# Input projection of a hybrid decoder step: one sweep over w_in for the u columns and the first token tile, with the bias products behind it

## The reference

```
h = rmsnorm(x);  [q | k | v | u] = h @ w_in          # 1024 x 2048
A: 8 heads x 64, dilated window attention (128,1), (512,4), (2048,16),
   T5 relative bias (32 buckets), branches merged by their denominators
B: u in 4 channel groups, trailing mean over 2/4/8/16 positions minus the token,
   then a 128 x 128 map per group and a scale per channel
x += [A | B] @ w_out
x += cross attention (4 heads x 256) into 256 memory tokens
x += top-4-of-32 mixture of experts (clamped SwiGLU)
y = rmsnorm(x)
```

## Time and profile before

| what | us |
|---|---|
| median of 3 runs | 1463.88 |
| lowest, highest | 1461.9, 1466.05 |
| profiled execution, its own time | 1460.94 |
| span in its profile | 1459.1 |
| TensorE busy | 1277.7 (88%) |
| VectorE busy | 479.7 (33%) |
| ScalarE busy | 238.5 (16%) |
| GpSimd busy | 65.2 (4%) |
| bytes moved by DMA | 562.83 MB, mean 386 GB/s |

### The profile page before, as it was taken

One profiled execution on the slowest core, in us unless ns is written; L12 is line 12 of the kernel. 1 busy time (PEld: TensorE's weight loads), 2 busy tenths in 40 slices (PEclk: granted clock), 3 DMA queues, 4 the chain that ended last, 5 costly groups with the idle time before them and its releaser, 6 DMA issues.

```text
span 1459.1 us, 16484 instructions
## 1 busy us (share of the span) xinstructions
PE 1277.7 (88%) x6397; PEld 532.2 (36%) x6397; DVE 479.7 (33%) x1025; ACT 238.5 (16%) x467; POOL 65.2 (4%) x64
## 2 busy tenths in 40 slices
PE   7985978899779499998999899988999999989986
PEld 4352333347554433333333233333333333333332
DVE  2038999531512621321321222212212232123124
ACT  2135343220321200110111010010010001001102
POOL 1010000002202400000000000000000000000000
PEclk9985988899989699999999999999999999999999
DMA  9988698799979979999999999999999999999993
GB/s 350 344 277 355 270 364 345 299 357 371 338 289 394 336 304 430 426 428 427 427 429 428 429 429 427 429 429 428 429 428 429 429 428 429 429 428 429 428 429 158
DMA packets 51212, 562.83 MB, mean 386 GB/s; under 512 B 6501, under 2 KB 8645, under 8 KB 20349
## 3 DMA queue, kind: packets, MB, share of 16 engines
q1 hardware_dynamic: 49589, 557.16, 93.6%
q0 software_dynamic: 1584, 5.13, 0.9%
HBM read 556.15 MB, written 73.28 MB: 431 GB/s over the span
## 4 chain that ended last, share of the span: by engine, by line
DMA 48%; PE 39%; DVE 10%; ACT 1%; issue 1%; SPq 0%; DVEq 0%; ACTq 0%
DMA wide<-in_w_gate_up 47%; PE bank L1777 12%; PE bank L1491 4%; PE bank L1384 3%; PE bank L1512 3%; PE bank L1801 2%; PE bank L1598 2%; PE bank L1534 2%; DVE small L1113 2%; DVE wide L1110 1%; PE bank L1400 1%; PE bank L1478 1%; PE bank L1586 1%; PE bank L1649 1%; DVE wide L1111 1%
## 5 line engine op out<-in xcount | busy, mean ns | idle before, releaser
L1777 PE MATMUL bank<-wide,att 128*64 128x512 f32 x2048 | 463.2, 596 | 59.2 <-DMA wide<-in_w_gate_up 59.2
L1777 PEld LDWEIGHTS bank<-wide,att 128*64 128x64 f32 x2048 | 139.8, 136 | 363.4 <-issue 228.5
L1801 PE MATMUL bank<-slim,att 128*64 128x512 f32 x1024 | 226.8, 595 | 0.0
L1306 DVE TENSOR_SCALAR att<-bank 128x512 f32<-128x512 f32 x32 | 22.1, 692 | 470.1 <-PE bank L1777 470.1
L1801 PEld LDWEIGHTS bank<-slim,att 128*64 128x64 f32 x1024 | 70.6, 137 | 152.2 <-issue 149.2
L1285 DVE TENSOR_TENSOR x<-x,bank 128x512 f32<-128x512 f32 x68 | 46.6, 686 | 236.6 <-PE bank L1759 226.4
L913 ACT ACTIVATE att<-att 128x512 f32<-128x512 f32 x32 | 20.2, 630 | 529.5 <-DVE att L1306 529.5
L1759 PE MATMUL bank<-tb,att 128*128 128x512 f32 (+1 forms) x192 | 84.7, 611 | 1.8 <-ACT tb L922 1.3
L922 ACT ACTIVATE tb<-bank 64x512 f32<-64x512 f32 x64 | 37.8, 591 | 234.1 <-PE bank L1801 233.7
L1512 PE MATMUL bank<-slim,ta 128*128 128x512 f32 x128 | 58.2, 608 | 0.0
L1113 DVE TENSOR_REDUCE small<-wide 128x24 f32<-128x1536 f32 x32 | 56.1, 1753 | 1.1
(11 more groups left out here) (269 smaller groups left out, 1132.6 us busy)
## 6 DMA issues: line engine op xcount, KB each, us to landing
wide<-in_w_gate_up SPq DMA_DIRECT2D x128, 2048.0 KB, 25.5
slim<-in_w_down SPq DMA_DIRECT2D x64, 2048.0 KB, 22.0
out_k_win_sample<-in_cache_k_win SPq DMA_DIRECT2D x16, 2044.0 KB, 23.7
out_v_win_sample<-in_cache_v_win SPq DMA_DIRECT2D x16, 2044.0 KB, 29.0
wide<-in_cache_k_win SPq DMA_DIRECT2D x16, 1024.0 KB, 9.1
wide<-in_cache_v_win SPq DMA_DIRECT2D x16, 1024.0 KB, 6.8
wide<-in_w_in SPq DMA_DIRECT2D x8, 1024.0 KB, 14.9
wide<-in_cache_mem_k SPq DMA_DIRECT2D x8, 1024.0 KB, 19.9
```

Source lines behind the costliest of these rows:

```text
L1777: ins = M(bk[half[h], :], rows[:, k, :], wide[:, k, c:c + 512], start=False, stop=k == KC - 1)
L1801: ins = M(bank_y[half[h], :], aT[:, f % 4, f // 4, :], slim[:, f, 512 * h:512 * h + 512], start=f == 0, stop=f == KC - 1)
```

## The change

- **Order of PE.** The transposes come first. Then one sweep over k makes the four `u` groups and the three `qkv` products of tile 0 together. Behind it stand `bias_w`, `bias_f`, `state`, all eight `toep`, `qkv` of the samples, and last `qkv` of tile 1. `trq`, `trk`, `fresh`, `utp`, `uts` and `pool` follow as before, without `state` between them.
- **ACT** copies in the order of the jobs. It makes `qrows` when the last product of tile 1 is there (they lie on columns of `wide` that hold `w_in`), then copies tile 1 out.
- **DVE** normalises and scales before it spreads the bias table. The pooling sums stand before the split of `qrows`.
- **`rbrep`** lies in `att` in place of `scr`, which the pooling sums use.
- **SP** loads x first and `w_in` before the bias constants. The windows wait for `qkv` of tile 1 in place of `u` 3. `COPIES` begins with 5, 4 in place of 7, 2: two copies, not four, stand between the Toeplitz table and the windows, and four, not two, behind the windows.

```diff
-        rbrep = scr[0:33, 0:1024].rearrange("p (h n) -> p h n", n=P)
+        rbrep = att[0:33, 4608:5632].rearrange("p (h n) -> p h n", n=P)
...
-        add("bias_w"), add("bias_f")
         for t in range(3):
             for h in range(2):
                 add("tr1", t, h)
-        for t in range(2):
-            for c in range(3):
-                add("qkv", t, c)
-            for h in range(4):
-                add("toep", 4 * t + h)
-        add("qkv", 2)
         for c in range(4):
             add("u", c)
+        for c in range(3):
+            add("qkv", 0, c)
+        add("bias_w"), add("bias_f"), add("state")
+        for h in range(HEADS):
+            add("toep", h)
+        add("qkv", 2)
+        for c in range(3):
+            add("qkv", 1, c)
...
-        COPIES = [7, 2, 1, 1, 1, 1, 1, 1, 2, 5, 2, 2, 6]
+        COPIES = [5, 4, 1, 1, 1, 1, 1, 1, 2, 5, 2, 2, 6]
...
         def _(sp):
-            load(sp, "ident", ident[:, :], i["c_ident"])
             for t, (t0, n) in enumerate(TOK):
...
+            load(sp, "ident", ident[:, :], i["c_ident"])
+            load(sp, "gcol", gcol[:, :, :], i["g_all"])
             load(sp, "rel", rb[0:BUCKETS, :], i["rel_bias"])
+            for k in range(KC):
+                sp.dma_start(wide[:, k, :], w_in[k]).then_inc(wide_in[k], 16)
             load(sp, "cbias", cb[:, 0:TOEP + 6 * P + 4 * NS], i["c_bias"])
...
-            b, use = place(("u", 3))
+            b, use = place(("qkv", 1, 2))
             sp.wait_ge(bank_full[b], use + 1)
...
+            rows_out(0)
+            ps, s = product(act, "state")
...
+            for h in range(HEADS):
+                ps, s = product(act, "toep", h)
...
+            read_out(act, "qkv", 2)
+            b_, use = place(("qkv", 1, 2))
+            act.wait_ge(bank_full[b_], use + 1)
             for c in range(3):
                 ins = A(qrows[NS * c:NS * c + NS, :], qn[0:NS, 2, :], ACT.Copy)
             ins.then_inc(qrows_in, 1)
+            rows_out(1)
...
+            for k in range(KC):
+                pe.wait_ge(wide_in[k], 16)
+                for c in range(4):
+                    ins = M(tu[c][0][:, 0:T], wide[:, k, 1536 + P * c:1536 + P * c + P], ta[:, k, :], start=k == 0, stop=k == KC - 1)
...
+                for c in range(3):
+                    ins = M(tk[c][0][:, :], ta[:, k, 0:P], wide[:, k, 512 * c:512 * c + 512], start=k == 0, stop=k == KC - 1)
...
```

More of the change, by code:

```diff
@@ L261, in build @@
         add("fresh", 0), add("fresh", 1)
-        add("state"), add("utp"), add("uts")
+        add("utp"), add("uts")
         for g in range(4):
             add("pool", g)
-        COPIES = [7, 2, 1, 1, 1, 1, 1, 1, 2, 5, 2, 2, 6]
+        COPIES = [5, 4, 1, 1, 1, 1, 1, 1, 2, 5, 2, 2, 6]
         ROUND_AT = {3: 1, 7: 2}
@@ L724, in _, with rows_out @@
                 root(t, n, x[0:n, t, :], hn[0:n, t, :])
[L726 to L729, removed]
+            def rows_out(t):
                 for c in range(3):
@@ L732, in _ @@
                     A(qkvn[:, c, t, :], ps[:, :], ACT.Copy, scale=HD ** -0.5 if c == 0 else 1.0).then_inc(s, 1)
[L733 to L736, removed]
             for c in range(4):
@@ L998, in _ @@
             ins.then_inc(s, 1)
[L999 to L1016, removed]
             dve.wait_ge(loaded["cfirst"], 16)
@@ L1038, in _ @@
                 dve.sem_inc(pooled, 1)
+            dve.wait_ge(qrows_in, 1)
+            for c in range(3):
+                V.tensor_copy(rowsel[NS * c:NS * c + NS, :], ident[NS * c:NS * c + NS, NS * c:NS * c + NS])
+            link(V.tensor_copy(qparts, qrows))
+            for c in (1, 2):
+                r = slice(NS * c, NS * c + NS)
+                link(V.tensor_tensor(qrows[r, :], qrows[r, :], qparts[r, :], ALU.subtract))
+                link(V.tensor_copy(qparts[r, :], qrows[r, :]))
+            link(V.tensor_tensor(qrows[64:96, :], qrows[64:96, :], qparts[64:96, :], ALU.subtract))
+            V.tensor_copy(qparts[64:96, :], qrows[64:96, :]).then_inc(qparts_in, 1)
+            for h in range(2):
+                ps, s = product(dve, "fresh", h)
+                dst = bfr[:, :, :, :].rearrange("p b t (c h) -> p h c (b t)", h=2)[:, h]
+                V.tensor_tensor(dst, dst, ps[0:NS, 0:128].rearrange("p (c q) -> p c q", q=NS), ALU.add).then_inc(s, 1)
             dve.wait_ge(loaded["toep"], 16)
@@ L1363, in _ @@
             ins.then_inc(s, 1)
[L1364 to L1391, removed]
+            pe.wait_ge(loaded["state"], 16)
+            ps, s = take(pe, "state")
+            ns = DEC_B * STATE
+            for c in range(4):
+                ins = TR(ps[:, ns * c:ns * c + ns], state[:, P * c:P * c + P], ident[0:ns, 0:ns])
+            ins.then_inc(s, 1)
+            for h in range(HEADS):
+                ps, s = take(pe, "toep", h)
+                M(ps[:, 0:TOEP], rbrep[:, h, :], cb[:, 0:TOEP], start=True, stop=True).then_inc(s, 1)
             ps, s = take(pe, "qkv", 2)
@@ L1396, in _ @@
             ins.then_inc(s, 1)
[L1397 to L1401, removed]
+            tk = [take(pe, "qkv", 1, c) for c in range(3)]
+            for k in range(KC):
+                for c in range(3):
+                    ins = M(tk[c][0][:, :], ta[:, k, P:2 * P], wide[:, k, 512 * c:512 * c + 512], start=k == 0, stop=k == KC - 1)
+                    if k == KC - 1:
+                        ins.then_inc(tk[c][1], 1)
             for t, (t0, n) in enumerate(TOK):
@@ L1414, in _ @@
                 ins.then_inc(s, 1)
[L1415 to L1420, removed]
             for c in range(4):
```

38 lines of the change are left out of this document (30 added, 8 removed).

## The result

Against 1462.39 us before (median of 8 runs, 1458.06 to 1466.05), the changed kernel took **1469.92 us** (median of 8, 1466.0 to 1472.0): a ratio of 1.0045, 95% interval 1.0027 to 1.0063, 7.5 us slower by the medians.

The account below looks back on a forecast made before the run. The compute chain up to the second expert's weights was taken as the bound. Projection ending 1.4 us later but the loop starting 2.4 us earlier gave 1461.5 us against the 1463.88 median, range 1456.0 to 1467.0.

Parts of the forecast that it names:

- Start of the sweep: Projection on TensorE: would start at 17.0 us, not 19.7, as VectorE normalises before spreading the bias table: -2.7 us.
- Cold start: First part of the projection: TensorE would begin at 1.2 GHz after idling, costing 2.0 us (0 to 3.4).
- Bias products at full clock: Bias products moved into TensorE's stream would take 3.4 us, against 5.8 us at half clock before.
- No cost of alternating `u` and `qkv`: In the projection sweep, alternating these two products was taken to cost nothing (up to 3 us).
- Pooling hidden: Pooling sums on VectorE, about 10 us, would run beside the `qkv` products and end before 80 us, at no cost.
- E: End of the last projection product on TensorE: 93.1 us before, forecast at 94.5 (about 91 to 98).
- The key window as the new wait in front of the loop: Before the sample loop: window landing at 115.7 us would replace pooling as the wait; loop starts at 118.3, 2.4 earlier.
- Toeplitz in one piece, -1.0: On TensorE, the eight Toeplitz products without alternation would save 1.0 us (0 to 2) of 7.3.
- Copies ... I take 0: Two more copies behind the windows take some 12 us of DMA slack; loss for sequence 2's keys taken as 0.
- rival B: Copies delay sequence 2's keys and sequence 1's values, losing 2 to 4 us: 1463.5 to 1465 us; chance 0.15.
- the base: The kernel before's end of the last projection product, read as 93.1 us from one profile, from which shifts were counted.
- Rival C: Pooling stores land late behind copies in flight, moving SP's wait and the loop by 15 us: 1478.9 us; chance 0.13.

Follow-up runs that it names:

- copies_7_2: Changed kernel with COPIES back at 7, 2 (four copies ahead of the windows, two behind): 1461.8 us, ratio 1.000 against the kernel before.
- padded_7_2: Changed kernel with COPIES at 7, 2 and Toeplitz products on 128 rows, the added rows zero: 1455.36 us, ratio 0.9956.
- toep_128_rows: Changed kernel with Toeplitz products reading 128 rows of other operands, leaving out the Toeplitz bias: 1464.31 us in a single run.
- toep_alternate: Changed kernel with Toeplitz products alternating with the samples' rows and tile 1, not in one piece: 1473.4 us, ratio 1.0085.
- before_copies_5_4: Kernel before with only the table of copies changed to 5, 4: 1462.32 us, ratio 1.0004.
- wfc_5_4: Changed kernel, COPIES at 5, 4, with window requests and all four copies ahead of SP's wait for the pooling stores: 1458.49 us, ratio 0.9976.

## Why the prediction was wrong

**Right.** Start of the sweep (16.84 against 17.0). Cold start: the granted clock is 0.50 from 17 to 20 us, and the first eight `u` products took 3.85 us and not 1.94, that is 1.9 for a term of 2.0. (Its upper bound, half of 7 us, came from no row; copies_7_2 lost some 3.3, with 4.18 and 3.77 us for the first two groups.) Bias products at full clock (2.77 + 0.41 for 3.4). No cost of alternating `u` and `qkv` (1.94 + 2.58 us in each later step). Pooling hidden, over at 70. SP awake, at the load ahead of the first window request, 12.1 us behind E (11.7; the prediction took that load for the request itself). The key window as the new wait in front of the loop, also that it was hidden before.

**Wrong, step "Toeplitz in one piece, -1.0", and with it the samples' rows at an unchanged price.** The Toeplitz products took 3.8 us more and not 1.0 less: 10.54 in place of 6.7 in the chain (the 7.3 of the earlier trace rows are busy time, in which neighbours overlap). Reading a cost of alternating from that row was not the fault. At half clock 10.54 us are, as an estimate, 5.3 us of work at the full clock, so one piece does pack better. The fault was to take the full clock for given once PE was busy, for every product behind the start of the sweep. A piece of bias, state and 33-row Toeplitz products kept it at 0.50 for 17 us, also over the first of the samples' rows (9.62 in place of 7.00). Against the sum these two are 4.8 and 2.6 us too much, all other terms together 1.9 too little, and the 5.5 us between E = 94.5 and 100.0 remain. padded_7_2 gives them back. The Trainium skill, TensorE: Matmul & The Clock Gate, Part 1, says that "activity releases the throttle". If activity is read as the profile's busy time, this trace does not agree: PE was busy all the time and the clock stayed low, and the same products on 128 rows released it.

**Wrong, step "Copies ... I take 0".** It cost 8.1 us (6.6 by the ratios). What happened is rival B, to which I gave 2 to 4 us and a chance of 0.15. The step took mean DMA shares of 0.43 and 0.45 as room for two copies. It did not reckon the row of DMAs through: six window halves, four copies and the two halves of the keys of sequence 2 are 16.4 MB, and SP asks for them in one order. From the first window request to the landing of these keys it was 48.3 us in the change (112.5 to 160.8), 48.4 in toep_128_rows (106.6 to 154.9) and 47.3 in toep_alternate (114.9 to 162.2). The keys are used 31.5 us behind the start of the loop (120.68 and 152.14 in the earlier trace rows). So, where all these transfers follow each other without a pause, the keys are late if the loop starts less than 16.8 us behind the request. In the change it starts 10.2 behind it, in toep_128_rows 10.0, in toep_alternate 10.2, and the late keys wait 6.75, 6.95 and 5.67 us. In before_copies_5_4 it starts 17.1 behind, in wfc_5_4 20.5: no wait. The prediction had both numbers, a request at 106.2 and a loop at 118.3, only 12.1 apart: by the 48.3 us measured since, the four copies were 4.7 us too much even at my own E. That the new kernel makes the window the last wait is the same fact as that it has no room behind it; I forecast the one and did not draw the other.

**Wrong, the base.** I set E = 93.1 as the start of before. Two other profiles have 95.2 and 96.0, with a cold start of the projection. Against these copies_7_2 loses 3.7 to 4.5 us at E (99.7) and wins 4.5 between E and the loop (23.0 in place of 27.6), which is why it comes out at 1.000 while its loop starts 2.0 us behind that of the earlier trace rows. Its 1461.8 us stand next to the forecast of 1461.5, but by luck: E was 5 us later than in the sum, the window landed 7.9 us after SP woke and not 9.5, and the base was 2 to 3 us too early.

**Rival C** did not happen in the change: the store took 2.5 us, for the two copies had landed by 94.2. The two runs that moved the Toeplitz table showed it at both sizes.

**Open.** In the two profiles the second expert's weights are asked for 10.3 us apart (519.67 and 529.96), while the medians are 7.5 apart. The two profiled executions are 11.1 us apart (1460.94 and 1472.0, the longest of its eight). The start of the projection can explain 1.9 to 2.4 us of such scatter; what the rest is, no run here tells. Nor does a run show what lets the clock fall at 57 to 60 us in every run with the new order: bias products of 8 columns, state transposes and the first Toeplitz products stand there together. The runs show what keeps it low.

## What to carry to other kernels

When a wait moves from an engine to a transfer, reckon the whole queue behind that transfer through to the next use of each item, in bytes at the rate that the trace shows; a mean DMA share of 0.4 says nothing on it. Two edits that each cost nothing alone can cost 7 to 8 us together, so undo them one at a time in both kernels. Look at the granted clock over pieces of products with few rows before collecting them in one place: among full-size products, as in the kernel before and in the second half of toep_alternate, the clock stayed at 1.00.

## What the runs showed of the hardware

TensorE, busy without a gap, was granted 0.50 of its clock, that is 1.2 GHz, for 17 us: over products with 33 of 128 rows (and 1 us of transposes), and for 5 us of products on 128 rows behind them. With 95 rows of zeros added the clock was back after some 3 us, and the Toeplitz products took 6.86 us in place of 9.95 (copies_7_2) to 10.54. A store of 64 KB took 1.9, 2.5, 8.8, 10.9 and 20.4 us to land, by what was moving when it was issued. A 1-MB load that takes 7.0 us in the kernel before took 21.1 behind windows and four 2-MB copies. And one profile of a start is one sample: the same six products took 2.77, 4.67 and 5.15 us in three executions of the same code.
